# Where the relative-bias tables of a hybrid decoder step are laid out: one change

## The reference

```python
def rel_bucket(dist):
    dist = jnp.maximum(dist, 0)
    max_exact = NUM_BUCKETS // 2
    scaled = jnp.log(jnp.maximum(dist, 1).astype(jnp.float32) / max_exact) / math.log(REL_MAX_DIST / max_exact)
    large = jnp.minimum(max_exact + (scaled * (NUM_BUCKETS - max_exact)).astype(jnp.int32), NUM_BUCKETS - 1)
    return jnp.where(dist < max_exact, dist, large)
...
    # group C; dist = q_pos - k_pos, one bias row for each head
    bias = jnp.moveaxis(bias_tab[rel_bucket(dist)], -1, 0)
    s = jnp.einsum('bqhmd,bkhmd->bmhqk', q, k) * (DC ** -0.5) + bias
...
    # group B, samples; for the dilations 1, 4 and 16
    bias = bias_tab[rel_bucket(dil * j)].T
    logits = jnp.einsum('bthd,btjhd->bhtj', q, kg) * scale + bias[None, :, None, :]
```

## Time and profile before

| what | value |
|---|---|
| time before, median of 3 runs | 3353.39 us (3353.12 to 3363.59) |
| the profiled execution's own time | 3384.77 us |
| its span, first to last instruction | 3383.1 us |
| mean granted TensorE clock over the span | 0.931 of full speed |
| PE busy | 3042.8 us, 90% of the span |
| DVE / ACT / POOL busy | 1525.7 / 666.3 / 149.0 us |
| chain that ended last | PE 82%, DVE 6%, DMA 3%, issue 3%, ACT 2% |
| bytes moved by q1 / q0 / q10 | 213.93 / 78.85 / 4.27 MB |

### The profile page before, as it was taken

The page is one execution under the profiler, slowest core; times in us unless marked ns, Lnnn a source line. Parts: engine busy times, 40 slices in busy tenths (PEclk is TensorE's granted clock), DMA queues, the critical chain, the costliest instruction groups (busy, mean ns, idle before and its releaser), DMA issues.

```text
span 3383.1 us, 46033 instructions
## 1 busy us (share of the span) xinstructions
PE 3042.8 (90%) x16606; PEld 2456.9 (73%) x16606; DVE 1525.7 (45%) x2834; ACT 666.3 (20%) x1259; POOL 149.0 (4%) x166
## 2 busy tenths in 40 slices
PE   2899999997778798999979999999877889899996
PEld 1788887887755476888868888788776555688885
DVE  3544534435544425445354454452454533444544
ACT  0111001213345211110011110122343541111100
POOL 0000000000033100000000000000002320000000
PEclk7899999998989788999989999999888996899998
DMA  5223222220057822321223222222103683232221
GB/s 148 63 75 87 60 78 63 75 62 29 2 169 214 230 75 64 85 86 51 85 80 87 80 56 78 72 75 62 54 0 104 205 240 94 84 87 80 57 78 61
DMA packets 363618, 299.05 MB, mean 88 GB/s; under 512 B 19427, under 2 KB 334973, under 8 KB 363171
## 3 DMA queue, kind: packets, MB, share of 16 engines
q1 hardware_dynamic: 340060, 213.93, 22.2%
q0 software_dynamic: 21888, 78.85, 7.4%
q10 hardware_dynamic: 1520, 4.27, 0.4%
HBM read 285.20 MB, written 11.81 MB: 88 GB/s over the span
## 4 chain that ended last, share of the span: by engine, by line
PE 82%; DVE 6%; DMA 3%; issue 3%; ACT 2%; DVEq 1%; ACTq 1%; SPq 0%; another core or an unknown queue 0%; POOL 0%; POOLq 0%
PE banks L634 29%; PE banks L690 16%; PE banks L746 12%; PE banks L657 5%; PE banks L1141 3%; PE banks L593 3%; PE banks L820 2%; PE banks L828 1%; PE banks L832 1%; DMA arena<-in_cache_v,layer_cache_rows 1%; DMA arena<-in_cache_win_v 1%; PE banks L989 1%; DVE normed_or_mixed L1580 1%; PE banks L1034 1%; PE banks L766 1%
## 5 line engine op out<-in xcount | busy, mean ns | idle before, releaser
L746 PE MATMUL banks<-normed_or_mixed,weight_slots 128*128 128x272 f32 x1792 | 416.9, 395 | 10.5 <-DVE normed_or_mixed L1580 10.5
L746 PEld LDWEIGHTS banks<-normed_or_mixed,weight_slots 128*128 128x128 f32 x1792 | 342.6, 191 | 83.2 <-DVE normed_or_mixed L1580 12.1
L634 PE MATMUL banks<-arena 128*128 128x272 f32 x1408 | 347.5, 401 | 14.9 <-DVE arena L1605 14.9
L634 PE MATMUL banks<-normed_or_mixed,arena 128*128 128x272 f32 x1408 | 337.0, 392 | 0.0
L634 PEld LDWEIGHTS banks<-arena 128*128 128x128 f32 x1408 | 274.0, 195 | 75.8 <-DVE arena L1605 17.7
L634 PEld LDWEIGHTS banks<-normed_or_mixed,arena 128*128 128x128 f32 x1408 | 267.5, 190 | 55.1
L1201 ACT ACTIVATE hidden_or_projected<-banks 128x1024 f32<-128x1024 f32 (+3 forms) x160 | 137.4, 864 | 255.1 <-PE banks L593 155.7
L690 PE MATMUL banks<-hidden_or_projected,keys_values_by_token 128*128 128x272 f32 x704 | 177.0, 392 | 0.0
L690 PE MATMUL banks<-arena,keys_values_by_token 128*128 128x272 f32 x704 | 169.2, 392 | 0.0
L690 PE MATMUL banks<-hidden_or_projected,weight_slots 128*128 128x272 f32 x704 | 169.2, 392 | 0.0
L593 PE MATMUL banks<-constants,hidden_or_projected 128*128 128x128 f32 (+2 forms) x880 | 137.4, 310 | 29.6 <-DMA hidden_or_projected<-in_x_sample 12.3
(11 more groups left out here) (370 smaller groups left out, 4393.1 us busy)
## 6 DMA issues: line engine op xcount, KB each, us to landing
weight_slots<-in_w_down SPq DMA_DIRECT2D x128, 256.0 KB
weight_slots<-in_w_in SPq DMA_DIRECT2D x28, 1024.0 KB
keys_values_by_token<-in_w_gate SPq DMA_DIRECT2D x48, 512.0 KB, 4.5
keys_values_by_token<-in_w_up SPq DMA_DIRECT2D x48, 512.0 KB, 4.7
weight_slots<-in_w_gate SPq DMA_DIRECT2D x40, 512.0 KB, 5.0
weight_slots<-in_w_up SPq DMA_DIRECT2D x40, 512.0 KB, 5.1
hidden_or_projected<-in_cache_win_k SPq DMA_DIRECT2D x112, 128.0 KB
weight_slots<-in_w_down SPq DMA_DIRECT2D x64, 192.0 KB
```

The costliest lines, as they stand in the source:

```text
L634: mm = pe.matmul(ps[:, bank, 0:HALF], weights[:, k, :], acts[:, k, :], start=first and k == 0, stop=k == 3, skip_group_check=True)
L746: mm = pe.matmul(half(bank + 2 * u, h), wslot[:, slot, at:at + 128], hT[:, k, h * HALF:(h + 1) * HALF], start=k == 0, stop=k == KD - 1)
```

## The change

The tables are still made by PE and DVE at the start, and written to DRAM once. All that follows moves from ACT's queue to GpSimd's, ahead of its loop over the layers. A second DRAM tensor, `skewed`, takes 128 copies of each head's table with rows of 640 elements at a pitch of 641, so that one load with a pitch of 640 gives all strips in the right row order; PE's flips and DVE's copies of them go away. A third one, `picked`, takes every sixteenth group of four elements. The sample rows go straight to `bias_c` and `bias_b`, in the order of the distances; DVE's reordering copies go away, and `logits` reads the bias with a step of four elements instead. The three additions for the samples' new keys move into the attention, at chunk 2, and so are done in both layers. The waits for the bias data (`in_strip`, `in_rows`) move to chunks 0 and 2 of the attention. `table` is placed inside `strips` instead of `work`. On PE the five table products use banks of their own. On DVE the token copies go ahead of the lambda vectors, and the table copies behind the sum of squares; on ACT the exponent of the lambda sums goes behind the squares.

```diff
@@ gpsimd, ahead of its loop over the layers
+            gp.wait_ge(s["setup_ev"], 11)
+            st(scratch[:, :], table[0:8, :], "table_out")
+            gp.wait_ge(s["table_out"], 16)
+            first = U_MAX - 384 - 127
+            st(bass.AP(tensor=skewed.tensor, offset=0, ap=[[128 * (SKEW + 1), 8], [SKEW + 1, 128], [1, SKEW]]),
+               bass.AP(tensor=scratch.tensor, offset=first, ap=[[U_TAB, 8], [0, 128], [1, SKEW]]), "table_out")
+            for step in range(T_S):
+                off = T_S - 1 - step
+                st(picked[step], bass.AP(tensor=scratch.tensor, offset=off, ap=[[U_TAB, 4], [16, 96], [1, 4]]), "table_out")
+                for b in range(4):
+                    st(bias_c[32 * b + step:32 * b + 32:4, :],
+                       bass.AP(tensor=scratch.tensor, offset=4 * U_TAB + off, ap=[[U_TAB, 4], [0, 2], [1, PAST + T_S]]), "in_rows")
+                st(bias_b[step:128:4, 0:512],
+                   bass.AP(tensor=scratch.tensor, offset=off + 1536, ap=[[0, 8], [U_TAB, 4], [1, 512]]), "in_rows")
+                st(bias_b[step:128:4, KEYS_B:KEYS_B + T_S],
+                   bass.AP(tensor=scratch.tensor, offset=off + PAST, ap=[[0, 8], [U_TAB, 4], [1, T_S]]), "in_rows")
+            gp.wait_ge(s["table_out"], 16 * (2 + T_S))
+            st(strips[:, :, :], bass.AP(tensor=skewed.tensor, offset=127, ap=[[SKEW, 128], [128 * (SKEW + 1), 8], [1, SEQ]]), "in_strip")
+            for step in range(T_S):
+                st(bias_b[step:128:4, 512:KEYS_B],
+                   bass.AP(tensor=picked.tensor, offset=step * 4 * (KEYS_B - 512),
+                           ap=[[0, 8], [KEYS_B - 512, 4], [1, KEYS_B - 512]]), "in_rows")
@@ tensor: the flips and the wait ahead of the layers
-            pe.wait_ge(s["in_strip"], 128)
-            for h in range(8):
...
-                pe.matmul(ps[:, 2 * (i % 2), :], C("flip"), strip_raw[:, h, :],
-                          start=True, stop=True).then_inc(s["setup_mm"], 1)
-            pe.wait_ge(s["setup_ev"], 19)
+            pe.wait_ge(s["setup_ev"], 6)
@@ scalar: all DMA issues of the setup
-            act.dma_start(scratch[:, :], table[0:8, :]).then_inc(s["table_out"], 16)
...
-                act.dma_start(strip_raw[:, h, :], src).then_inc(s["in_strip"], 16)
...
+            act.wait_ge(s["lam_sums"], 1)
+            act.activation(lam_sum, lam_sum, ACT.Exp).then_inc(s["lam_exp"], 1)
@@ vector: setup
-                cp(strips[:, h, :], ps[:, 2 * (i % 2), :]).then_inc(s["setup_ev"], 1)
-            dve.wait_ge(s["in_rows"], 16 * 5 * T_S)
...
-            cp(bias_c[:, 0:PAST].rearrange("p (c r g) -> p c g r", c=4, r=4),
-               win_c[:, 0:PAST].rearrange("p (c g r) -> p c g r", c=4, r=4))
@@ vector: logits()
-                    stt(dst[:, here], ps[:, 2, 0:here.stop - here.start], scale, bias[:, here], ALU.mult, ALU.add)\
-                        .then_inc(s["s_log"], 1)
+                    stt(dst[:, here].rearrange("p (r g) -> p r g", r=4),
+                        ps[:, 2, 0:here.stop - here.start].rearrange("p (r g) -> p r g", r=4), scale,
+                        bias[:, here].rearrange("p (g r) -> p r g", r=4), ALU.mult, ALU.add).then_inc(s["s_log"], 1)
@@ vector: attention(), chunks 0 and 2
                     if n == 0:
+                        dve.wait_ge(s["in_strip"], 16)
...
                     if n == 2:
+                        dve.wait_ge(s["in_rows"], 16 * 7 * T_S)
+                        alone(dve)
+                        for g in range(2):
+                            dve.tensor_tensor(bias_cn[:, g, :].rearrange("p (b t) -> p b t", b=8),
...
```

More of the change, by code:

```diff
@@ L38 @@
 KEYS_B = 896
+SKEW = 640
 CH_C, CH_B = 32, 14
@@ L139, with trunk @@
 )
-def trunk(nc, A, O, scratch):
+def trunk(nc, A, O, scratch, skewed, picked):
     where, n_const = columns()
```

86 lines of the change are left out of this document (30 added, 56 removed).

## The result

| what | before | changed kernel |
|---|---|---|
| median of 4 runs each on one chip | 3358.49 us (3353.12 to 3364.07) | 3335.09 us (3334.81 to 3335.52) |
| ratio, 95% interval | | 0.9919 (0.9899 to 0.9939) |
| same comparison on another chip | 3359.89 us, 9 runs | 3332.76 us, 5 runs: 0.9922 (0.9908 to 0.9935) |

The kernel is 23 to 27 us faster. The profiled execution whose rows stand above took 3384.77 us, 31 more than its median, and can't be set beside the new one stage by stage.

The account below looks back on a forecast made before the run. Bias transfers, not PE, were taken to hold the first FFN matmul; moving it from 90.1 to 60.9 us gains 29.2, less 2.8 in the attention: 26.4 off 3353.4 gives 3327 us, range 3317 to 3342.

Parts of the forecast that it names:

- What bounds the setup: First 100 us: bias transfers, not PE, hold the first FFN matmul at 90.13 us; moving it moves the end equally.
- Candidate 1: Setup: DVE's own work, possibly the next thing late once the old wait goes, done at 33.3 us.
- Candidate 2: Setup: the page table's last load lands at 45.4 to 47.9 us, so DVE asks for weights at 48.2 to 50.7.
- Candidate 3: Setup: the second half of the first gate weights, issued at 36.2 us, lands undisturbed at 48.1.
- The contention term: Setup: the skewed copy delays the first gate weights by 0 to 7.0 us, taken as 5.6, to 53.7.
- The stepped logits: Attention: 20 logits operations reading bias with a four-element step cost 0 to 8.5 us; a third, 2.8, was taken.
- The additions: Attention, chunk 2: three additions per layer ahead of the prompt logits, 0 to 1.2 us in all, taken as 0.
- At least 10 us to spare for each later load: First FFN: weight loads after the first arrive at least 10 us before DVE wants them.
- no change: Something unseen holds the first matmul, or the FFN's second or third load gives everything back: 3353 us, chance 4%.
- few-engines case: Setup: the skewed copy loads part of the engines, first weights land at 66.2 us; gain 13.9, 3339 us, chance 20%.
- Full cost of the step: Attention: all 8.5 us of the stepped read plus 1.2 of additions land on the path; 3334 us, chance 12%.
- Starving: Setup: queue rivalry lands the first gate weights at 88 us, after 82.9; 3361 us, slower, chance 4%.

Follow-up runs that it names:

- pages_late: Changed kernel with DVE's page-table wait and page-number operations behind the first FFN, and the twelve loads behind GpSimd's transfers: 3322.42 us, 0.9879; another chip 3320.07 us, 0.9878.
- pages_wait_late: Changed kernel with only DVE's page-table wait and page-number operations moved behind the first FFN, the loads staying on SP: 3336.13 us, ratio 0.9921.
- contig: Changed kernel with the logits reading their bias in a row again, so the samples' results are not the reference's: 3331.01 us, ratio 0.9915.
- triple_skew: Changed kernel with the copy to the skewed tensor done three times, twice into a tensor nobody reads: 3351.29 us.

## Why the prediction was right, and which of its steps were not

The forecast was 3327 us, faster, in 3317 to 3342; it came out faster, at 3335.

- **What bounds the setup, and that its gain reaches the end: right.** Putting back the wait alone undid everything, and moving the first matmul by 12.9 us (pages_late against pages_wait_late) moved the total by 13.7.
- **Candidate 1, DVE's own work at 33.3: right.** The table copies ended at 32.8, and in pages_late DVE came to the weights out of that work.
- **Candidate 2, the page table: right.** The wait ended at 45.16, a little before the 45.4 to 47.9 forecast, and the weights were asked for at 48.74 (48.2 to 50.7); DVE needed 3.58 us between them, not 2.76.
- **Candidate 3, gate weights at 48.1 undisturbed: right**, within 0.3 us in pages_wait_late.
- **The contention term, 5.6 us of 0 to 7.0: mis-sized; it was 0.** The step that failed is that the table's write would land 3.4 or 9.1 us after issue, with the copy under way before the weights. It took 11.6, as it stood beside the page table's loads, and the copy began when the first weights were nearly in. So the first matmul ran at 56.0, not 60.9, and the setup's gain was 33.8, not 29.2. That the page table's loads held back the copy was luck: the prediction counts them as a wait of DVE and nowhere as a brake on the copy.
- **The stepped logits, 2.8 us of 0 to 8.5: mis-sized; it was about 5.** DVE worked 7.3 us longer on them (20.8 against 13.5 us in all), and the attentions are 5.1 to 5.5 us longer with the step in three pairs of kernels on the same chip. A third of the upper bound was too little, it was six tenths. The step that failed is that PE's larger share would cover most of a DVE delay: of the 7.3 us some 5 came through (with the scatter of the profiles, 2 to 8).
- **The additions, 0: right**, as far as it shows (contig).
- **At least 10 us to spare for each later load: wrong.** It was 0.9 us for the first up weights and 3.4 for the second gate weights, and three copies made both negative. The first matmul came 4.9 us earlier than forecast, and with it the moments at which DVE wants them. The up weights, for which the prediction gives no landing, took 25.2 us in place of 12.2, and the 30.0 us of the earlier trace rows was not the worst: this time the load took 32.0. So the contention of the copy was real, but it fell on the loads behind the one to which the prediction gave it, and that nobody waited was a matter of 0.9 us.
- **The sum.** Its terms make 33.8 - 5 = 29, the spans say 27.2 and the two comparisons of medians 23 and 27, against 26.4 forecast: two errors, +4.6 and -2.3, go against each other, and that they did is luck. Of the 8.1 us by which 3327 was missed, 5.1 are the base (3358.5 in the comparison of the result, not 3353.4) and 3.0 the gain (23.4, not 26.4). The base was the median of three runs that had two of them at the low end, 3353.1 and 3353.4; in the four later comparisons the kernel before took 3360 to 3363. In the chances, no change with the rest of the few-engines case makes 0.09, where the text has 0.08, and slower 0.04, where it has 0.05.
- **The rivals.** Few engines: its premise fits, its price did not come. The trace has the start and length of every packet. The copy's 512 packets of 5.1 KB run eight at a time: in pages_late, where no weights moved beside it, eight were under way for 81% of its time and nine for most of the rest; in the changed kernel eight for 47% and hardly ever more. The three copies of triple_skew together reached 16. The Trainium skill (DMA: Bandwidth & Descriptors, Rules for kernel authors) says that a small outermost dimension confines a transfer to as many engines; this copy, whose source has eight heads there, agrees with it. But the first weights were in before the copy ran, so its 3339 us has nothing to do with the 3335 measured. Full cost of the step: the measured cost lies between, about 5 of 8.5. Starving: the mechanism is real, but it met the loads behind the first gate weights, and ended 0.9 us before anyone waited; triple_skew shows it in earnest, with 13.2 us of waiting. No change: excluded by the interval of the ratio.

## What to carry to other kernels

Ask of a removed stage which of its waits moved rather than which of its instructions went: here the flips and strip copies were hidden behind the wait for the rows, the reordering copies were worth about 3 us (from 77.19 to 80.15 in the earlier trace rows), and the place of one wait was worth 43 us, 9 of which paid for a slower layout. When a wait goes, go down the list of what it hid to the end, since the next one (twelve small loads ahead of the weights in SP's queue) can be moved as cheaply as the first; and count the room of every load behind the first one, as the narrowest here had 0.9 us. Give the operands of a repeated operation their order once, on an idle engine and at a time when its neighbours have time to spare, rather than by a step in every use.

## What the runs showed of the hardware

- **Two queues share the engines packet by packet, not byte by byte.** While both had work, q0 and q1 moved 385 and 385 packets, and with narrower rows 540 and 539; the weights' packets of 0.5 KB (0.20 MB / 385) beside the copy's of 5.1 KB (1.97 MB / 385) got a tenth of the bytes. The Trainium skill (DMA: Bandwidth & Descriptors, Queues, rings and completion order) says that each engine goes round its queues packet by packet; these counts agree. Whether weights read in longer rows would stand up better was not tried.
- **A step cost DVE time on SBUF, read or write, and not on its read of PSUM.** 512 elements took 0.69 us without a step, 1.05 to 1.12 with 16 bytes on one SBUF side, 0.68 to 0.69 with 16 bytes on the PSUM side. The Trainium skill (SBUF — State Buffer, Door 1: The DMA port swizzle) gives SBUF lines of 16 bytes, with a penalty for each access that crosses to a new one, and PSUM lines of 8, where it speaks of slower matmuls. For SBUF the rows agree, and they set the price at 0.7 to 0.8 ns an element; for DVE's read of PSUM, of which the sentence doesn't speak, they show none.
- **Many tiny packets on one queue held up a transfer on another.** From 36 to 40 us of the changed kernel the page table's packets took 9.8% of the engines' time and moved 0.00 MB, and yet the table's write, issued on another queue at 33.09, moved nothing in this stretch and landed 11.6 us after issue, in place of 4.2 to 5.1 without these loads. Why so little work holds it is not shown:

```profile
q1 hardware_dynamic: 769, 0.00, 9.8%
```
